# Value-page loads moved to one queue and re-ordered against the output projection of a hybrid decoder step

## What is computed

```
proj = xn @ w_in                       # q k v z xbc dt
attn = rmsnorm(attend(q, k, v))        # samples: two cache pages of keys and of values each
y    = rms(ssd(x, dt, b, c) * silu(z)) # two groups of heads
out  = concat([attn, y]) @ w_out
x    = x + out;  x = x + peer_ffn(rmsnorm(x))
```

## Time and profile before

| | us |
|---|---|
| median of 3 runs | 1171.94 |
| their range | 1170.41 to 1173.0 |
| the profiled execution, its own time | 1171.42 |
| its span, first to last instruction | 1169.7 |
| PE busy | 1144.1 |
| DVE, POOL, ACT busy | 768.0, 738.3, 604.8 |

### The profile page before, as it was taken

How to read it: one execution, slowest core, us unless ns; L and a number is a source line. 1 busy time by engine, 2 the same in 40 slices (tenths; PEclk the granted TensorE clock), 3 DMA queues, 4 the chain that set the end, 5 groups by cost and what they waited for, 6 DMA issues and landing times.

```text
span 1169.7 us, 24328 instructions
## 1 busy us (share of the span) xinstructions
PE 1144.1 (98%) x7599; PEld 1011.1 (86%) x7599; DVE 768.0 (66%) x1686; ACT 604.8 (52%) x1388; POOL 738.3 (63%) x610
## 2 busy tenths in 40 slices
PE   8999999789899999999999999999999999999997
PEld 7888787569788999999999999998888888888876
DVE  6787676952399996003899999984454466665534
ACT  3355554843355555564555544445555555555545
POOL 0032221737365998998666667666677798788754
PEclk9999999998999999999999999999999999999999
DMA  7578766784453766656554444445666697688643
GB/s 240 177 236 277 225 216 197 244 316 145 144 161 93 219 186 187 185 159 199 144 143 140 143 144 139 143 145 154 189 189 189 188 327 265 231 275 294 190 153 108
DMA packets 108668, 225.13 MB, mean 192 GB/s; under 512 B 12754, under 2 KB 21570, under 8 KB 108074
## 3 DMA queue, kind: packets, MB, share of 16 engines
q1 hardware_dynamic: 104706, 210.50, 58.0%
q0 software_dynamic: 2944, 10.49, 2.5%
q10 hardware_dynamic: 936, 3.14, 0.7%
HBM read 215.80 MB, written 8.19 MB: 192 GB/s over the span
## 4 chain that ended last, share of the span: by engine, by line
PE 72%; issue 1%; DVE 0%; POOL 0%; ACT 0%; DVEq 0%; POOLq 0%; ACTq 0%
PE bank L1747 31%; PE bank L1777 30%; PE bank L1757 5%; PE bank L1700 2%; PE bank L1712 1%; PE bank L1724 1%; PE bank L1797 0%; PE bank L1814 0%; POOL hl L1640 0%; DVE acts L2173 0%; PE bank L1805 0%; ACT acts L1983 0%; POOL hl L1625 0%; PE bank L1832 0%; PE bank L1790 0%
## 5 line engine op out<-in xcount | busy, mean ns | idle before, releaser
L1625 POOL TENSOR_TENSOR hl<-ring,hl 128x512 fp32r<-128x512 f32 x448 | 587.1, 1321 | 184.3 <-ACT hl L1863 176.5
L1863 ACT CAST hl<-ring 128x512 fp32r<-128x512 f32 x512 | 317.1, 620 | 290.5 <-PE bank L1777 156.8
L1747 PE MATMUL bank<-split,hl 128*128 128x256 f32 x3072 | 378.4, 282 | 0.4 <-ACT hl L1863 0.3
L1747 PEld LDWEIGHTS bank<-split,hl 128*128 128x128 f32 x3072 | 366.2, 188 | 0.8 <-issue 0.5
L1777 PE MATMUL bank<-hl,split 128*128 128x512 f32 x1524 | 353.6, 394 | 0.0
L1777 PEld LDWEIGHTS bank<-hl,split 128*128 128x128 f32 x1524 | 286.0, 188 | 67.7 <-issue 0.9
L528 PE MATMUL pj<-xn,ring 128*128 128x264 f32 x672 | 156.7, 388 | 0.7 <-ACT proj L833 0.7
L2143 DVE TENSOR_TENSOR split<-acts,split 128x256 fp32r<-128x256 f32 x128 | 130.5, 1044 | 37.9 <-ACT split L1959 33.7
L528 PEld LDWEIGHTS pj<-xn,ring 128*128 128x128 f32 x672 | 125.0, 190 | 24.2 <-issue 4.4
L2150 DVE TENSOR_TENSOR hl<-ring,hl 128x512 fp32r<-128x512 f32 x64 | 46.6, 729 | 116.7 <-ACT hl L1863 116.7
L2109 DVE TENSOR_SCALAR bv<-bkey,ig 128x130 f32<-128x130 f32 x256 | 86.0, 394 | 0.0
(11 more groups left out here) (369 smaller groups left out, 1113.7 us busy)
## 6 DMA issues: line engine op xcount, KB each, us to landing
ring<-in_uv SPq DMA_DIRECT2D x256, 256.0 KB
ring<-in_v_rows SPq DMA_DIRECT2D x256, 256.0 KB
ring<-in_w_ring SPq DMA_DIRECT2D x76, 512.0 KB, 4.3
room<-in_cache_k SPq DMA_DIRECT2D x64, 128.0 KB, 2.7
hs<-in_state_ssm SPq DMA_DIRECT2D x8, 512.0 KB, 5.6
out_ssm_s<-hs SPq DMA_DIRECT2D x8, 512.0 KB, 6.3
acts<-x_rows SPq DMA_DIRECT2D x8, 512.0 KB, 5.4
room<-in_cache_v SPq DMA_DIRECT2D x12, 256.0 KB, 5.7
```

What stands on the lines that cost most here:

```text
L1625: nc.gpsimd.tensor_tensor(hl[:, r % HL, 1], raw[:, r], hl[:, r % HL, 0].bitcast(F32), ALU.subtract).then_inc(lo_done, 1)
L1747: mm = nc.tensor.matmul(out, hl[:, r % HL, m, k * P:(k + 1) * P], split[:, x, kk, 0:TP], start=(kk == 0 and n == 0), stop=(kk == KD - 1 an ...
L1863: nc.scalar.copy(hl[:, r % HL, 0], raw[:, r]).then_inc(hi_done, 1)
```

## The change

- SP issues all eight value units. POOL has no transfers any more.
- One more place: `proj`'s part X0, free when the SSD outputs and sample outputs of all eight steps are made (`y_done`, `ys_done`). Value unit 5 goes there.
- SP's order becomes key unit 7, value units 1, 0, tiles 44, 45, unit 5, tile 46, units 2, 3, 4, tile 47, the last state, the table, units 6, 7, the stores, tile 48 and on.
- On PE key units 6 and 7 come ahead of `attend(6)`; value units 4 to 7 alternate with the output halves of tiles 44 to 47; the two matmuls for the squares, both narrow gathers and the spreading follow behind the half of tile 47.
- On ACT and DVE pair 7 of the prompt and the SSD roots are moved behind the sample steps, and casts of pieces 6 to 9 stand ahead of `probs_out(7)` and `attended(7)`. The second `values_kept` and `sample_factors` move ahead of the prompt's variance, the low remainders of the attention behind the samples' sum.

```diff
+        val_homes.append(part(proj[:].rearrange("p k n -> p (k n)"), X0 * NT, SIDE, D // 2))
-        V_HOME = (2, 3, 4, 0, 1, 2, 4, 0)
+        V_HOME = (2, 3, 4, 0, 1, 5, 4, 0)
...
+                    elif n == 5:
+                        sp.wait_ge(y_done, KD)
+                        sp.wait_ge(ys_done, KD)
                     else:
-                        sp.wait_ge(unit_used, {4: KU, 5: KU + 1, 6: KU + 3, 7: KU + 4}[n])
+                        sp.wait_ge(unit_used, {0: KU - 2, 3: KU - 1, 4: KU, 6: KU + 3, 7: KU + 4}[n])
...
                             values(1)
+                            values(0)
...
                 tile(N_IN)
+                tile(N_IN + 1)
+                values(5)
+                tile(N_IN + 2)
                 values(2)
-                tile(N_IN + 1)
+                values(3)
                 values(4)
-                for i in range(N_IN + 2, N_IN + RING):
-                    tile(i)
+                tile(N_IN + 3)
                 state_out(KD - 1)
...
-                for n in range(5, VU):
+                for n in (6, 7):
                     values(n)
...
-                    if c == KD - 2:
-                        values(0)
...
-                values(3)
...
+                    if c == KD - 1:
+                        key_unit(KU - 2)
+                        key_unit(KU - 1)
...
                 out_half(N_IN + 1, 1, 1, True, False)
+                value_unit(5)
                 turn_probs(KD - 1)
-                value_unit(5)
-                attend(KD - 1)
+                value_unit(6)
                 pe.wait_ge(v6_masked, 2)
                 out_half(N_IN + 2, 2, 1, True, False)
+                attend(KD - 1)
+                value_unit(7)
+                out_half(N_IN + 3, 3, 1, True, False)
...
                 values(0)
-                value_unit(6)
-                out_half(N_IN + 3, 3, 1, True, False)
-                value_unit(7)
                 values(1)
...
+                out_high(6, 8)
                 probs_out(KD - 1)
+                out_high(8, 10)
                 attended(KD - 1)
...
-                out_high(6, 8)
+                act.wait_ge(unit_used, KU + 6)
...
-                out_high(8, 10)
```

More of the change, by code:

```diff
@@ L481, in _ @@
                     sums.then_inc(st_done, 1)
[L483 to L492, removed]
                 pool.wait_ge(st_done, KD)
-                pool.wait_ge(ptab_in, 16)
                 for c in range(KD - 1):
-                    if c == KD - 2:
-                        values(0)
                     pool.wait_ge(o_copied, 2 * c + 2)
@@ L697, in _ @@
                         group_sums(0)
-                        key_unit(KU - 2)
-                        key_unit(KU - 1)
                         group_sums(1)
@@ L997, in _ @@
                     else:
+                        spread(c)
                         squares(0)
@@ L1005, in _ @@
                     else:
-                        spread(c)
                         squares(1)
@@ L1033, in ssd_high @@
                     nc.scalar.copy(mixr[:, KD + 4 * n:KD + 4 * n + 4], mix[:, KD + 4 * n:KD + 4 * n + 4]).then_inc(mix_hi, 1)
-                group_root(0)
                 for b in range(NQ):
                     sample_exps(b)
+                group_root(0)
+                act.wait_ge(sum_s, 2)
+                out_high(0, 2)
                 act.wait_ge(pt6_ready, 1)
@@ L1041, in _ @@
                 group_root(1)
-                out_high(0, 2)
                 ssd_high(0)
-                exps(KD - 1)
+                ssd_high(1)
+                out_high(2, 4)
                 act.wait_ge(diffs6, 2)
                 nc.scalar.activation(s6[:, 4:6], s6[:, 4:6], ACT.Exp, scale=SCALE).then_inc(rates6, 1)
-                ssd_high(1)
-                out_high(2, 4)
+                exps(KD - 1)
                 out_high(4, 6)
                 normal(KD - 1)
+                out_high(6, 8)
                 probs_out(KD - 1)
+                out_high(8, 10)
                 attended(KD - 1)
@@ L1061, in _ @@
                     nc.scalar.copy(mixr[:, 4 * n:4 * n + 4, 0:TP], mix[:, 4 * n:4 * n + 4, 0:TP]).then_inc(mix_hi, 1)
-                out_high(8, 10)
                 act.wait_ge(att_s, 1)
                 nc.scalar.activation(sq_att[:, :, TP:NT], mix[:, 0:KD, TP:NT], ACT.Square).then_inc(sq_l, 1)
-                out_high(10, 11)
+                out_high(10, 12)
                 act.wait_ge(var_l, 1)
                 nc.scalar.activation(rr[:, 0, TP:NT], rr[:, 0, TP:NT], ACT.Sqrt).then_inc(root_l, 1)
-                out_high(11, 12)
                 act.wait_ge(mixed_l, 1)
@@ L1343, in _ @@
                 nc.vector.tensor_tensor(qk6[:], proj[:, Q0:Q0 + KD, TP:NT], proj[:, K0:K0 + KD, TP:NT], ALU.mult).then_inc(qk6_ready, 1)
-                group_var(0)
                 dve.wait_ge(unit_used, KU)
@@ L1347, in _ @@
                 nc.vector.tensor_scalar(s6[:, 1], s6[:, 0], -SCALE, None, ALU.mult).then_inc(max6, 1)
+                group_var(0)
                 group_var(1)
@@ L1375, in ssd_scaled @@
                                                        in1=tmp[:, n], op0=ALU.mult, op1=ALU.mult).then_inc(mixed_s, 1)
-                ssd_scaled(0)
-                masked(KD - 1)
                 dve.wait_ge(own_ready, 1)
@@ L1381, in _ @@
                 sample_rates()
+                ssd_scaled(0)
                 ssd_scaled(1)
@@ L1391, in _ @@
                 mix_low(1, 2, lows[2], slice(0, NT)).then_inc(mix_lo, 1)
-                recips(KD - 1)
                 mix_low(2, 3, lows[3], slice(0, NT)).then_inc(mix_lo, 1)
@@ L1401, in values_kept @@
                                                 ALU.mult).then_inc(v6_masked, 1)
+                masked(KD - 1)
                 values_kept(0)
+                recips(KD - 1)
+                sample_factors()
+                values_kept(1)
                 dve.wait_ge(pt_copied, 2 * KD)
@@ L1408, in _ @@
                 nc.vector.reciprocal(rr[:, 0, 0:TP], rr[:, 0, 0:TP]).then_inc(var_p, 1)
-                sample_factors()
                 dve.wait_ge(root_p, 1)
@@ L1413, in _ @@
                                                    in1=rr[:, 0, 0:TP], op0=ALU.mult, op1=ALU.mult).then_inc(mixed_p, 1)
-                values_kept(1)
-                for n in (0, 1):
-                    mix_low(n + 3, n, lows[n], slice(0, TP)).then_inc(mix_lo, 1)
                 dve.wait_ge(spread6, 1)
@@ L1424, in _ @@
                 nc.vector.tensor_tensor(mix[:, 0:KD, TP:NT], tmp6, o6[:], ALU.add).then_inc(att_s, 1)
+                for n in (0, 1):
+                    mix_low(n + 3, n, lows[n], slice(0, TP)).then_inc(mix_lo, 1)
                 dve.wait_ge(sq_l, 1)
```

## The result

The median of four runs is 1178.30 us (1177.61 to 1178.57). The kernel before, run beside it, has 1171.18 us (1169.35 to 1173.0). The ratio is 1.006 with a 95% interval of 1.0042 to 1.0077: slower, by 7.1 us, where the forecast said slower by about 4 and gave 1167.0 to 1178.0 as its range. The median lies 0.3 us above that range. The profiled execution of after took 1178.38 us (6.96 more than that of before), its span is 1176.5 us.

The account below looks back on a forecast made before the run. PE, busy 98% of the span, was taken as the bound, with about 14 us of gaps and slow clock to win. Squares at 259.5 plus 18.8 us put T at 278.3, 4.0 later: 1175.4 us, range 1167.0 to 1178.0.

Parts of the forecast that it names:

- the hold: ACT's casts of tile 48 wait for its landing and keep back the copy and square; PE waits 7.1 us.
- T: Start of PE's long run of output halves: 274.30 us before, forecast 278.3; all later PE work is the same.
- a worse form: Slower still: slow SP issues in all late units and last half partly at 1.2 GHz, 1178 us; chance 0.12.
- Part 1, the queue: SP's queue: seven units at 4.40 us, tiles, state and table take 35.9 us; store of k at 245.3.
- Part 2, the units: Value units on PE: unit 0's 4.80 us gap goes, PE finishes the half of tile 47 at 252.4, before 257.0.
- the 4.6 that the forecast saw at that half: PE's gain at the end of tile 47's half, 252.4 instead of 257.0; reaches T only without the wait.
- the change does what it says: Rival: tile 48 lands by about 250, no wait before the squares; 1164.1 us, or 1167 with slow clock; chance 0.16.
- Part 3, the hold,: ACT's cast of tile 48 ahead of the copy: tile lands at 257.1, squares at 259.5, PE waits 7.1 us.
- the rival that the tile overtakes the stores: Rival on the DMA queue: loads overtake stores, tile 48 lands by about 250, no PE gap; chance 0.16.
- Part 4, squares to T,: PE from squares to the long run, narrow matmuls at half clock: 18.8 us, T 4.0 us later than before.
- The chain on DVE: Squares, reciprocal, scalings, remainders, short steps: 10.6 us, ending at 270.1, hidden since PE reaches the small sum at 275.0.
- QUEUE: Theory from the experiments: eight more transfers on SP make all that stands behind them late.

Follow-up runs that it names:

- experiment 1: Changed kernel with ACT's casts of pieces 8 and 9 (tile 48) put back behind the root of the prompt's last pair: 1170.86 us, ratio 0.9992 to the kernel before.
- experiment 2: Changed kernel with the three stores issued behind tile 51, ACT's cast of tile 48 still ahead of the copy: 1169.57 us, ratio 0.9984.
- experiment 4: Kernel before, with only the casts of pieces 6 to 9 moved ahead of the copy of the attention output on ACT: 1186.16 us, ratio 1.0122.
- experiment 7: Experiment 6 with value unit 3 alone issued by POOL: 1166.05 us, ratio 0.996.
- experiment 5: Experiment 2 with DVE's two low remainders made ahead of the wait for the spreading, as before the change: 1169.64 us, ratio 0.9981.
- experiment 6: Experiment 5 with the output half of tile 48 moved between the two narrow gathers on PE: 1170.36 us, ratio 0.9989.
- experiment 10: Experiment 5 (narrow matmuls in one row) with value unit 3 issued by POOL: 1167.05 us, ratio 0.9963.
- experiment 9: Changed kernel with only value unit 3 given back to POOL, casts and stores left in place: 1175.88 us, ratio 1.0032.
- experiment 3: Changed kernel with value units 0 and 3 issued by POOL again, cast still ahead of the copy: 1175.36 us, ratio 1.003.
- experiment 11: Experiment 10 with value unit 6 on POOL as well, between two low parts: 1166.41 us, ratio 0.9954.

## Why the prediction was right in kind and too small in size

The direction and the mechanism came as forecast. Three of the signs it named are there: the cast begins after 12.98 us of idle time ended by a transfer (10 or more were named), PE idles 6.00 us before L789 (7), and the clock is 0.50 under the narrow matmuls. Experiments 1, 2 and 4 show that the hold carries the loss. The times it named came 2 to 3.3 us late: the store of k at 247.25 (245), the cast at 259.25 (257), and T at 281.59 (278.3), so that this execution took 1178.38 us and not 1175.4.

That the measured time comes so near the top of the range is luck. The top stood for a worse form, with slow issues in the late units and a last half partly at 1.2 GHz. Neither came: the issues of units 6 and 7 spanned 3.69 and 3.86 us (4.36 was the slow case), and the last half ran in 3.14 us. Other terms made up the difference.

**Part 1, the queue, is the term that failed most.** The step that failed is "I take 4.40 us for a unit, the reads of the page table included". From 209.46 to 247.25 SP took 37.8 us, not 35.9. Less 1.92 for the tiles, 0.47 for the state and 3.19 for the table, seven units took 32.2, or 4.60 each: +1.4 us. The table took 3.19 instead of 2.7: +0.5. The store of k left at 247.25 instead of 245.3, no sooner than before.

The 4.40 was counted from the first issue of unit 7 on, and so left out the time ahead of that issue, in which SP reads the first page number (the same 0.76 us stands between the issues of a unit: four of 0.33 us span 3.60). Before, the row ahead of unit 7 is

```profile
237.91 4.00 SPq L385 DMA_DIRECT2D xn<-in_cache_v  x4
```

It ends at 241.91, 0.77 us before unit 7 begins at 242.68. In after six of the seven units have 0.77 to 0.81 us ahead of their first issue and unit 6 has 1.16, together 5.85 us. Their four issues span 3.61 to 4.16 us, 26.3 in all, which is 3.76 on the mean and less than the 4.36 of the unit that the forecast took. So 0.84 us a unit was left out and 0.64 was priced too high, and 0.20 remains, seven times. The 1.6 us that I had allowed for slow issues in units 6 and 7 were not what was missing. What makes the span of a unit vary wasn't tried.

**Part 2, the units.** The forecast had unit 3 at 231 and unit 4 in time, so that nothing would wait. PE waited for units 3, 4 and 6 (1.87, 2.10, 0.84 us), and the clock fell within 239 to 240. The half of tile 47 ended at 255.6 instead of 252.4. As forecast this changed nothing with the hold there. This fits experiments 1 and 2, which are free of the hold and yet gain only 0 to 2 us and not the 4.6 that the forecast saw at that half, and experiment 7, where these waits are gone and 3.4 to 4.3 us more are gained. The rival "the change does what it says" would not have given 1164 either. The idle 2.17 us before unit 0 and the slow clock under units 0 and 1 (1.91 and 1.69 us) were not in the sum either, though the forecast put unit 0 rightly at 225.9.

**Part 3, the hold,** was right to 0.2 us from its own start: store of k to cast 12.0 us (11.85 forecast), cast to squares 2.4 (2.4). The Trainium skill (DMA: Bandwidth & Descriptors, Queues, rings and completion order) says that completions are not in order per issuing engine, from which the forecast made the rival that the tile overtakes the stores. No run shows that: the tiles needed 9.9 us behind the stores, and from issue to cast 6.1, 6.5 and 7.0 us in experiments 2, 5 and 6 with the stores behind them.

**Part 4, squares to T,** took 19.95 us instead of 18.8. The squares took 1.83 (1.2 forecast, a price that supposed part of them at the full clock), gathers and spreading 10.10 (9.1), the half of tile 48 with the short wait behind it 4.83 (5.2), the small sum 0.21 (0.1), the last half 2.98 (3.2): +1.15. The 9.1 was three times a spreading that in the earlier trace rows ran only "mostly" at 1.2 GHz; wholly at 1.2 GHz a gather of 16 takes 3.4. The chain on DVE was misread as well. The forecast let the low remainders follow the scalings and end at about 270; in after they stand behind the samples' sum, which waits for the spreading, so they begin at 274.63 and the small sum waits 0.29 us for DVE. Together 1.95 + 0.15 + 0.04 + 1.15 = 3.29, which is the whole miss.

**What a second issuer saves.** The Trainium skill (Trainium Kernel Development and Optimization, Key Constraints) says that several issuers save only issue time. The runs agree, and here issue time is on the path: by the medians one unit moved back to POOL is worth 4.3 us without the hold (experiments 6 and 7), 2.6 in the row form (5 and 10, on two chips, with intervals that overlap) and 2.4 with the hold (9). Two units moved were worth no more (3 and 11).

**What stays open.** Traces of kernels that are alike up to there differ in where the clock falls within 225 to 245 us, and by some 3.5 us in when SP issues unit 1; neither was worked out. Whether HOLD and QUEUE add up was not tried on one chip. That DVE is the bound at the small sum in experiments 6 and 7, by 1.73 and 1.85 us, was read from the waits and not tested alone.

## What to carry to other kernels

On ACT, a step placed early that waited for a late transfer held back everything behind it, however independent. Before moving a cast ahead, find when its tile is issued and what stands ahead of that issue, large stores above all. When transfers are gathered on one queue, add up every issue from the last wait to the load that is needed, since the sum of issue times may set when it leaves. Count each one from the end of the issue before it, so that the read of its address is in the price. And price a gap ahead of narrow matmuls above its own length (here 6.0 us idle and about 3 us more at T), since they didn't bring the clock back.

## What the runs showed of the hardware that I had not expected

- Narrow matmuls keep PE busy in the trace (1.00 within 266 to 267 us of after) without bringing the clock back, as the forecast had supposed from the earlier trace rows: it stayed at 0.50 from 260 to 276 through 48 matmuls of 4 and 16 columns, and rose some 3 us into a half of 264 columns. A gather of 32 takes 6.83 us so, and 3.63 where the clock had not fallen.
- Narrow matmuls without any gap ahead end with a fall too. In experiment 10 PE has no idle time between 250 and 265 us, and the clock falls at the end of the spreading (258.78 to 260.86 us). Stretches of 2 us with the columns of the earlier trace rows:

```profile
258.00:260.00 2.00, 2.00 (x20) 2.00 (x20) 1.72 (x5) 0.25 (x1) 0.00 (x0) 1.00 1.01 415
260.00:262.00 2.00, 2.00 (x13) 2.00 (x13) 2.00 (x5) 1.47 (x2) 0.00 (x0) 0.61 0.32 127
262.00:264.00 2.00, 2.00 (x11) 2.00 (x11) 2.00 (x3) 0.62 (x1) 0.00 (x0) 0.54 0.01 4
```

- A tile of 512 KB takes 9.9 us from issue to landing behind 2.6 MB of stores on its queue, and from issue to cast only 6.1 to 7.0 when issued ahead of them (tile 48 in experiments 2, 5, 6), or 4.6 in experiment 7. The fourth tile of experiment 2 took 9.2 us even so.
- The clock fell within 225 to 226 us of after although PE had been idle for at most 2.17 us, behind 64 matmuls of 2 columns and 4 of 128; that PE runs units at half speed there (1.91 us) is a cost that no wait view shows.
